# Second block, attention: the last head rows' 1/rms moved behind the second and third heads' maxima, and its spreading products one and two heads later

## The chip, the cores and the metric

One core of one Trainium2 chip runs the whole program. The metric is device time in microseconds (us) of one execution; less is better. TensorE multiplies matrices into PSUM (PE in the profile, its weight loads are PEld), VectorE (DVE) and ScalarE (ACT) do the elementwise work and the activations, GpSimd (POOL) makes the low halves of split weights, and SyncE (SP) issues the loads of the weight stream.

## The reference

Two transformer-like blocks run on a sequence of 256 rows with 1024 columns. The change lies in the second block's attention, whose 16 heads are 64 wide: 8 "forgetting" heads (fox) and 8 "stick breaking" heads (sb).

```python
q, k, v = heads(proj...)                  # (16 heads, 256, 64)
q_fox = rms_norm_2(q[:, :8], fox_q_g)     # x * rsqrt(mean(x*x) + eps) * g, per head and row
k_fox = rms_norm_2(k[:, :8], fox_k_g)
...
logits = q_fox @ k_fox.T * scale + cum_f[q] - cum_f[k]      # causal
p = softmax(logits);  o_fox = p @ v
o = concat([o_fox, o_sb]) @ w_out
h = h + o
```

So before any logit of a fox head can be made, the head's query and key must have been divided by their root mean square, 8 query and 8 key heads in all, held as blocks of two heads (128 partitions).

## The kernel before

Each engine has its own instruction queue, written out by hand in program order, and the engines meet at counting semaphores. Work is staged: first block, its feed-forward part, then the second block's attention (its part here is from about 645 us to 750 us of the span), and then the feed-forward and convolution parts.

In the attention, TensorE projects 16 blocks `j` of queries and keys (`project`). The square sums of blocks 4g to 4g+3 are collected as 8 rows (`head_sums`, L1038, group g). Their 1/rms is made in two parts: ScalarE forms a first guess by logarithm and exponential (`row_rsqrt(g)`, L1588 and L1591), and VectorE improves it in one Newton step of four operations on 8x256 elements (`row_rstd(g)`, L1761 to L1765). The result is split into a high part by ScalarE (`heads_hi(g)`, L1596) and a low part by VectorE (`heads_lo(g)`, L2276). TensorE then spreads the rows over 128 partitions, one product of 256 columns per block (`spread_rstd(i)`, L1048, block i of 16), and VectorE multiplies block i by it (`finish_qk(i)`, L2283). Group 3, the one that the change moves, belongs to blocks 12 to 15, and these are the queries and keys of fox heads 4 to 7.

The spreads of blocks 12 and 14 write one PSUM bank, those of 13 and 15 another. `spread_rstd(14)` therefore waits for `finish_qk(12)`, and `spread_rstd(15)` for `finish_qk(13)`.

Each fox head h then goes through this chain:

- `fox_scores(h)`, TensorE: two query tiles, products L1147, L1149, L1151 and L1153. It waits for its blocks (`qk_fin`) and for the exponentials of head h-2.
- `fox_maximum(h)`, VectorE: two reductions, L2346.
- `fox_exps(h)`, ScalarE: two activations with sums, L1651.
- `fox_even(h)`, VectorE: a reciprocal (L2352) and two multiplications (L2355).
- `fox_transposes(h)`, TensorE: three transposes, L1165.
- `fox_turned(h)`, VectorE: a copy out of PSUM, L2363.
- `fox_values(b)`, TensorE: the product with v for heads 2b and 2b+1, L1174 and L1178.

`sb_values(b)` (L1124, L1128) is the corresponding product of the sb heads. `out_hi(n)` on ScalarE (L1642) and `out_lo(n)` on VectorE (L2339) split an output block. `out_half(n, half)` on TensorE (L546 to L548, 12 products) is half of the output projection of block n. `out_half(0, 0)` waits until all 16 blocks are finished (`qk_fin` 26), since it writes the banks of the spreads. It stands behind `fox_scores(4)` in TensorE's queue, and `fox_values(0)` stands behind it.

Four waits are the ones to keep in mind:

```python
# spread_rstd(i)
pe.wait_ge(S["heads_split"], 1 + g)
if i > 8: pe.wait_ge(S["qk_fin"], 10 + fin_before(i) + 1)
# fox_transposes(h)
pe.wait_ge(S["fox_even"], 2 * h + 2)
# out_half(n, 0)
pe.wait_ge(S["qk_fin"], 26)
```

Of the kernel before, what the change touches and what calls it, by code (L numbers as in the profile page):

```python
# [135 lines left out]
def build(nc, xc_d, ccol_d, params_d, const_d, const1_d, const2_d, wgate_d, wf_d, stream_d, out_d):  # L136
# [3 lines left out]
    with ctx:  # L140
# [351 lines left out]
        def q_bank(j):  # L492
            return 2 + j if j < 2 else 4 + j % 2
# [26 lines left out]
        def fin_out(i):  # L520

            return PS[:, 4 + i % 2, T:2 * T] if i < 8 else PS[:, 0 if i < 12 else i % 2, 0:T]

        def fin_before(i):

            return i - 1 if i < 13 else i - 2
# [17 lines left out]
        def _(pe):  # L544
# [496 lines left out]
            def spread_rstd(i):  # L1041

                g, b = i // 4, i % 4
                pe.wait_ge(S["heads_split"], 1 + g)
                pe.wait_ge(S["heads_ready"], 4)
                if i > 8:
                    pe.wait_ge(S["qk_fin"], 10 + fin_before(i) + 1)
                pe.matmul(fin_out(i), spread2[b // 2][:, P * (b % 2):P * (b % 2) + P], head_rows[g],  # L1048
                          start=True, stop=True).then_inc(S["fin_bc"], 1)
# [106 lines left out]
            def fox_transposes(h):  # L1156

                pe.wait_ge(S["fox_even"], 2 * h + 2)
                if h >= 2:
                    pe.wait_ge(S["fox_pt"], h - 1)  # L1160
                else:
                    pe.wait_ge(S["evac_v"], v_before + 20)
                    pe.wait_ge(S["qk_fin"], 10 + 8)
                for k in range(3):
                    mm = pe.transpose(PS[:, 4 + h % 2, P * k:P * k + P], f_P[h % 3][:, P * k:P * k + P], ident)  # L1165
                mm.then_inc(S["ft_done"], 1)
# [16 lines left out]
            def out_half(n, half):  # L1183

                wait_rest(pe, S_OUT2 + n)
                pe.wait_ge(S["t2_lo"], n + 1)
                if half == 0:
                    pe.wait_ge(S["qk_fin"], 26)
                else:
                    pe.wait_ge(S["fox_exp"], 16)  # L1190
                for m in range(4 * half, 4 * half + 4):
                    mm = mm3(PS[:, m // 2, (m % 2) * T:(m % 2) * T + T], *w(S_OUT2 + n, m), *out_rows(n),
                             n == 0 and m % 2 == 0, False)
                if half == 1:
                    mm.then_inc(blk_done, 1)
# [24 lines left out]
            for h in range(2, 11):  # L1220
                if h < 10:
                    fox_transposes(h - 2)
                if h < 8:
                    fox_scores(h)
                if h == 2:
                    sb_values(3)
                if h in (2, 3):
                    spread_rstd(2 * h + 8)
                    spread_rstd(2 * h + 9)
                if 4 <= h < 8:  # L1230
                    out_half(h - 4, 0)
                if h in (8, 9):
                    out_half(h - 8, 1)
                if h in (4, 6, 8, 10):
                    fox_values((h - 4) // 2)
# [34 lines left out]
        def _(act):  # L1270
# [322 lines left out]
            def heads_hi(g):  # L1593

                act.wait_ge(S["rq_done"], 3 + g)
                act.activation(head_rows[g][0:8, :], PS[0:8, g % 2, T:2 * T], ACT.Copy).then_inc(S["heads_hi"], 1)  # L1596
# [47 lines left out]
            def fox_exps(h):  # L1644

                act.wait_ge(S["fox_max"], 2 * h + 2)
                if h >= 3:
                    act.wait_ge(S["ft_done"], h - 2)
                for qt, cols in enumerate(FOX_Q):
                    u = 2 * h + qt  # L1650
                    act.activation(f_P[h % 3][:, cols], PS[:, 2 + h % 2, cols], ACT.Exp, bias=foxnm[:, u:u + 1],  # L1651
                                   accum_out=foxsum[:, u:u + 1]).then_inc(S["fox_exp"], 1)

            for j in range(18):
                if j == 17:
                    fox_exps(0)
                if j in (5, 9, 13, 17):
                    row_rsqrt((j - 5) // 4)
                if j == 17:
                    sb_weights(7)  # L1660
                    heads_hi(3)
                if 0 <= j - 9 < 8:
                    sb_logs(j - 9)
                if 0 <= j - 10 < 7:
                    sb_weights(j - 10)
                if j in (13, 15, 17):
                    out_hi((j - 13) // 2)
                if j < 16:
                    act.wait_ge(blk_done, S_ATT2 + KC + j + 1)
                    if 6 <= j < 14:  # L1670
                        act.wait_ge(S["fin_bc"], j - 5)
                    if j >= 2:
                        act.wait_ge(S["st_done"], 10 + j - 1)
                    act.activation(sqr2[j % 2], PS[:, q_bank(j), 0:T], ACT.Square).then_inc(S["qk_sq"], 1)
                    if j in (5, 9, 13):
                        heads_hi((j - 5) // 4)
                    if j == 3:
                        fox_operands()
                    if j == 4:
                        act.wait_ge(S["f_add"], 1)  # L1680
                        act.activation(fr[1][0:8, :], fr[0][0:8, :], ACT.Abs).then_inc(S["f_act"], 1)
                        act.wait_ge(S["f_act"], 1)
                        act.activation(fr[1][0:8, :], fr[1][0:8, :], ACT.Exp, scale=-1.0).then_inc(S["f_act"], 1)
                        act.wait_ge(S["f_act"], 2)
                        act.activation(fr[1][0:8, :], fr[1][0:8, :], ACT.Ln, bias=1.0).then_inc(S["f_act"], 1)
                    splits_upto(S_ATT2 + KC + j + RING)


            for h in range(1, 12):
                if h < 8:  # L1690
                    fox_exps(h)
                if h == 3:
                    out_hi(3)
                if h in (5, 7, 9, 11):
                    out_hi(4 + (h - 5) // 2)
# [31 lines left out]
        def _(dve):  # L1727
# [537 lines left out]
            def row_rstd(g):  # L2265
                dve.wait_ge(S["st_done"], 10 + 4 * g + 4)
                r = PS[0:8, g % 2, T:2 * T]
                newton(rr2[1][0:8, :], r, fr[2][0:8, :], r, PS[0:8, g % 2, 0:T],
                       1.0 / HD, S["rq_done"], lambda x: dve.wait_ge(S["row_act"], 4 + 2 * g + 2))
                dve.wait_ge(S["rq_done"], 3 + g)  # L2270

            def heads_lo(g):

                dve.wait_ge(S["heads_hi"], 1 + g)
                r = PS[0:8, g % 2, T:2 * T]
                dve.tensor_tensor(head_rows[g][32:40, :], r, head_rows[g][0:8, :].bitcast(f32), ALU.subtract)\  # L2276
                   .then_inc(S["heads_split"], 1)
# [3 lines left out]
            def finish_qk(i):  # L2281
                dve.wait_ge(S["fin_bc"], i + 1)
                dve.scalar_tensor_tensor(q2[:, i, :], q2[:, i, :], gains[2 * (i // 8) + i % 2], fin_out(i),  # L2283
                                         ALU.mult, ALU.mult).then_inc(S["qk_fin"], 1)
# [50 lines left out]
            def out_lo(n):  # L2335

                dve.wait_ge(S["t2_hi"], n + 1)
                hi, lo = out_rows(n)
                dve.tensor_tensor(lo, PS[:, 6 + n % 2, 0:T], hi.bitcast(f32), ALU.subtract).then_inc(S["t2_lo"], 1)  # L2339

            def fox_maximum(h):

                for qt, cols in enumerate(FOX_Q):
                    u = 2 * h + qt
                    dve.wait_ge(S["fs_done"], 2 * h + 2)
                    dve.tensor_reduce(foxnm[:, u:u + 1], PS[:, 2 + h % 2, cols], AX.X, ALU.max, negate=True)\  # L2346
                       .then_inc(S["fox_max"], 1)
# [52 lines left out]


            finish_qk(11)
            row_rstd(3)
            fox_maximum(1)
            heads_lo(3)
            for h in range(2, 12):
                if h < 10:
                    fox_turned(h - 2)
                if h == 2:
                    fox_maximum(h)  # L2410
                    out_lo(2)
                if h < 9:
                    fox_even(h - 1)
                if 3 <= h < 8:
                    fox_maximum(h)
                if h in (2, 3):
                    finish_qk(2 * h + 8)
                    finish_qk(2 * h + 9)
                if h == 3:
                    out_lo(3)  # L2420
                if h in (5, 7, 9, 11):
                    out_lo(4 + (h - 5) // 2)
# [205 lines left out]
```

## Time and profile before

| | |
|---|---|
| median of 3 runs | 1244.06 us (1242.25 to 1244.53) |
| profiled execution, its own time | 1248.76 us |
| profiled execution, span from first to last instruction | 1247.0 us |
| TensorE busy | 1235.5 us, 99% |
| VectorE busy | 737.0 us, 59% |
| ScalarE busy | 670.9 us, 54% |
| GpSimd busy | 712.3 us, 57% |
| mean granted TensorE clock over the span | 0.994 |

A busy share is the time in which at least one instruction of the engine is in flight. TensorE's matrix products are pipelined, so it counts as busy also where it is not at its peak. The granted clock is 1.00 at 2.4 GHz and 0.50 at 1.2 GHz.

### The profile page before, as it was taken

The numbers are of one execution on the slowest core, as the hardware profiler recorded it, in microseconds if no ns is written. First come the engines' busy times: TensorE is split into PE (matmuls) and PEld (weight loads), VectorE is DVE, ScalarE is ACT, GpSimd is POOL, SyncE is SP. The second block draws the span as 40 slices with busy tenths as digits, with TensorE's granted clock in tenths as the row PEclk, the third lists the DMA queues.
The fourth block names the chain that finished last, engine by engine and source line by source line (L and its number), as shares of the span: only waits on it lengthen the run. The fifth ranks groups of instructions, "written<-read, shape, count | busy, mean of one in ns | idle before, by whom it ended". The sixth has DMA issues, their size and how long they took to land.

```text
span 1247.0 us, 24363 instructions
## 1 busy us (share of the span) xinstructions
PE 1235.5 (99%) x8666; PEld 1109.5 (89%) x8666; DVE 737.0 (59%) x1619; ACT 670.9 (54%) x1205; POOL 712.3 (57%) x308
## 2 busy tenths in 40 slices
PE   8999999999999999999999999999999999999998
PEld 5788889877799999999888779999999999999998
DVE  5796667456542666665626644766666334766665
ACT  6333334455544755555755526666666445666663
POOL 5476553342258656558675306655675986665563
PEclk9999999999999999999999979999999999999999
DMA  9978542231146455456463204554564654555451
GB/s 342 369 257 303 203 152 69 87 110 58 36 135 181 140 188 201 168 185 220 144 186 121 85 1 122 183 186 170 199 217 132 195 185 150 172 202 179 174 218 52
DMA packets 58188, 208.11 MB, mean 167 GB/s; under 512 B 6640, under 2 KB 7808, under 8 KB 58112
## 3 DMA queue, kind: packets, MB, share of 16 engines
q1 hardware_dynamic: 57888, 206.56, 48.7%
q8 instruction: 49, 0.80, 0.3%
q0 software_dynamic: 224, 0.52, 0.1%
q14 instruction: 27, 0.22, 0.1%
HBM read 206.01 MB, written 1.05 MB: 166 GB/s over the span
## 4 chain that ended last, share of the span: by engine, by line
PE 93%; DVE 3%; DMA 1%; ACT 1%; issue 1%; POOL 1%; SPq 0%; DVEq 0%; ACTq 0%
PE ps L546 18%; PE ps L547 18%; PE ps L548 18%; PE ps L575 13%; PE ps L577 6%; PE ps L597 2%; PE ps L599 2%; PE ps L600 2%; PE ps L822 2%; PE ps L627 1%; PE ps L893 1%; PE ps L919 1%; PE ps L908 1%; DMA raw<-in_stream 1%; PE ps L1153 1%
## 5 line engine op out<-in xcount | busy, mean ns | idle before, releaser
L333 POOL TENSOR_TENSOR wlo<-raw,whi 128x1024 fp32r<-128x1024 f32 x287 | 695.7, 2438 | 506.6 <-ACT whi L1283 467.1
L1283 ACT ACTIVATE whi<-raw 128x1024 fp32r<-128x1024 f32 x338 | 353.2, 1054 | 110.7 <-PE ps L548 43.4
L546 PE MATMUL ps<-H,whi 128*128 128x256 f32 (+3 forms) x1312 | 386.5, 295 | 1.4 <-DVE H L1816 1.1
L547 PE MATMUL ps<-H,whi 128*128 128x256 f32 (+3 forms) x1312 | 377.5, 288 | 0.0
L548 PE MATMUL ps<-H,wlo 128*128 128x256 f32 (+3 forms) x1312 | 377.3, 288 | 0.0
L546 PEld LDWEIGHTS ps<-H,whi 128*128 128x128 f32 (+1 forms) x1312 | 250.4, 191 | 14.3 <-issue 10.0
L547 PEld LDWEIGHTS ps<-H,whi 128*128 128x128 f32 (+1 forms) x1312 | 250.9, 191 | 2.5
L548 PEld LDWEIGHTS ps<-H,wlo 128*128 128x128 f32 (+1 forms) x1312 | 250.3, 191 | 2.5
L575 PE MATMUL ps<-H,whi 128*128 128x512 f32 x672 | 238.9, 398 | 0.0
L2205 DVE SCALAR_TENSOR_TENSOR arena<-ps,sm,arena 128x256 f32<-128x256 f32 (+2 forms) x264 | 127.5, 483 | 103.7 <-ACT arena L1541 96.1
L577 PE MATMUL ps<-H,wlo 128*128 128x256 f32 x672 | 188.7, 281 | 0.0
L546 PE MATMUL ps<-dh,whi 128*128 128x256 f32 x584 | 165.4, 283 | 0.5 <-DVE dl L2214 0.5
L547 PE MATMUL ps<-dl,whi 128*128 128x256 f32 x584 | 165.2, 283 | 0.0
L548 PE MATMUL ps<-dh,wlo 128*128 128x256 f32 x584 | 165.2, 283 | 0.0
L575 PEld LDWEIGHTS ps<-H,whi 128*128 128x128 f32 x672 | 126.3, 188 | 29.5
L577 PEld LDWEIGHTS ps<-H,wlo 128*128 128x128 f32 x672 | 127.0, 189 | 0.0
L546 PEld LDWEIGHTS ps<-dh,whi 128*128 128x128 f32 x584 | 111.1, 190 | 2.8 <-POOL wlo L333 0.9
L548 PEld LDWEIGHTS ps<-dh,wlo 128*128 128x128 f32 x584 | 111.3, 191 | 0.0
L547 PEld LDWEIGHTS ps<-dl,whi 128*128 128x128 f32 x584 | 111.3, 191 | 0.0
L1541 ACT ACTIVATE arena<-ps,sm 128x256 f32<-128x256 f32 x132 | 66.1, 500 | 16.6 <-DVE ps L2195 12.8
L1533 ACT ACTIVATE arena<-ps 128x256 f32<-128x256 f32 x84 | 32.3, 385 | 62.4 <-PE ps L577 62.3
L2167 DVE TENSOR_TENSOR wlo<-raw,whi 128x1024 fp32r<-128x1024 f32 x51 | 62.3, 1222 | 1.5 <-issue 0.3
(337 smaller groups left out, 1496.3 us busy)
## 6 DMA issues: line engine op xcount, KB each, us to landing
raw<-in_stream SPq DMA_DIRECT2D x386, 512.0 KB, 4.2
X<-in_xc SPq DMA_DIRECT2D x4, 512.0 KB, 6.0
out_y<-X SPq DMA_DIRECT2D x8, 128.0 KB, 1.9
kx<-in_const SPq DMA_DIRECT2D x1, 512.0 KB, 8.6
params<-in_params SPq DMA_DIRECT2D x1, 344.0 KB, 5.1
kx<-in_const POOLq DMA_DIRECT2D x1, 256.0 KB, 4.3
k<-in_const POOLq DMA_DIRECT2D x1, 129.0 KB, 5.6
k<-in_const SPq DMA_DIRECT2D x1, 128.0 KB, 5.1
```

Source lines behind the costliest of these rows:

```text
L333: pool.tensor_tensor(wlo[:, slot, :], raw[:, rslot, :], whi[:, slot, :].bitcast(f32), ALU.subtract).then_inc(rest_done[0], 1)
L546: pe.matmul(out, lh, rh, start=start, stop=False, skip_group_check=True)
L547: pe.matmul(out, lh, rl, start=False, stop=False, skip_group_check=True)
L548: return pe.matmul(out, ll, rh, start=False, stop=stop, skip_group_check=True)
L575: pe.matmul(PS[:, bank, :], wh_, F[:, k, :, :].rearrange("p h n -> p (h n)"), start=k == 0, stop=False, skip_group_check=True)
L577: mm = pe.matmul(PS[:, bank, T:2 * T], wl_, Fh[:, k, :], start=False, stop=k == KC - 1, skip_group_check=True)
L597: pe.matmul(out, hi[:, k, tok], wh_, start=k == 0 and first, stop=False, skip_group_check=True)
L1283: act.activation(whi[:, s % RING, :], raw[:, r % RING, :], ACT.Copy).then_inc(hi_done, 1)
L1533: act.activation(tc, PS[:, 4 + 2 * slot + j, T:2 * T], ACT.Copy).then_inc(S["half_out"], 1)
L1541: act.activation(tc, PS[:, 4 + 2 * slot + j, at:at + T], ACT.Identity, bias=bias, scale=taps_of(f)[:, slot, 3 * j:3 * j + 1]).then_inc(S[" ...
L2167: dve.tensor_tensor(wlo[:, s % RING, :], raw[:, RAW_OF_W[s] % RING, :], whi[:, s % RING, :].bitcast(f32), ALU.subtract).then_inc(rest_done ...
L2205: dve.scalar_tensor_tensor(tc[:, lo:hi], u[:, src:src + hi - lo], taps_of(f)[:, slot, 3 * j + 1 + n:3 * j + 2 + n], tc[:, lo:hi], ALU.mult ...
```

## The change

The Newton step of group 3 (`row_rstd(3)`) leaves its place ahead of `fox_maximum(1)` on VectorE and goes behind `fox_maximum(2)` and `out_lo(2)`. `heads_hi(3)` on ScalarE goes from ahead of `fox_exps(1)` to behind `fox_exps(2)`. `heads_lo(3)` goes to head step h = 3, behind `fox_turned(1)`. On VectorE `fox_even(1)` now stands ahead of `fox_maximum(2)`. On TensorE the spreads of blocks 12 and 13 go from step 2 to the same place in step 3, behind `fox_scores(3)`, and those of 14 and 15 from behind `fox_scores(3)` to step 4, between `fox_transposes(2)` and `fox_scores(4)`. `finish_qk(12)` and `(13)` go from step 2 to step 3, behind `fox_maximum(3)`; `finish_qk(14)` and `(15)` go from step 3 to step 4, behind `fox_turned(2)`. No instruction is added or removed.

```diff
 # TensorE
             for h in range(2, 11):
                 if h < 10:
                     fox_transposes(h - 2)
+                if h == 4:
+                    spread_rstd(14)
+                    spread_rstd(15)
                 if h < 8:
                     fox_scores(h)
                 if h == 2:
                     sb_values(3)
-                if h in (2, 3):
-                    spread_rstd(2 * h + 8)
-                    spread_rstd(2 * h + 9)
+                if h == 3:
+                    spread_rstd(12)
+                    spread_rstd(13)
                 if 4 <= h < 8:
                     out_half(h - 4, 0)
 # ScalarE
                 if j == 17:
                     sb_weights(7)
-                    heads_hi(3)
...
             for h in range(1, 12):
                 if h < 8:
                     fox_exps(h)
+                if h == 2:
+                    heads_hi(3)
                 if h == 3:
                     out_hi(3)
 # VectorE
             finish_qk(11)
-            row_rstd(3)
             fox_maximum(1)
-            heads_lo(3)
             for h in range(2, 12):
                 if h < 10:
                     fox_turned(h - 2)
-                if h == 2:
-                    fox_maximum(h)
-                    out_lo(2)
+                if h == 3:
+                    heads_lo(3)
+                if h == 4:
+                    finish_qk(14)
+                    finish_qk(15)
                 if h < 9:
                     fox_even(h - 1)
-                if 3 <= h < 8:
+                if h < 8:
                     fox_maximum(h)
-                if h in (2, 3):
-                    finish_qk(2 * h + 8)
-                    finish_qk(2 * h + 9)
+                if h == 2:
+                    out_lo(2)
+                    row_rstd(3)
                 if h == 3:
+                    finish_qk(12)
+                    finish_qk(13)
                     out_lo(3)
```

## Rows read from the trace of the kernel before

**Rows 1.** The page: span, busy TensorE, and the chain that ended last, by engine.

```profile
span 1247.0 us, 24363 instructions
PE 1235.5 (99%) x8666; PEld 1109.5 (89%) x8666; DVE 737.0 (59%) x1619; ACT 670.9 (54%) x1205; POOL 712.3 (57%) x308
...
PE 93%; DVE 3%; DMA 1%; ACT 1%; issue 1%; POOL 1%; SPq 0%; DVEq 0%; ACTq 0%
```

**Rows 2.** Windows (from:to, length, busy us by engine with counts, granted clock, DMA).

```profile
706.00:719.00 13.00, 12.84 (x74) 8.80 (x73) 10.20 (x27) 6.87 (x20) 2.36 (x1) 1.00 0.14 41
...
720.00:734.00 14.00, 14.00 (x56) 10.73 (x56) 6.09 (x20) 2.10 (x9) 0.00 (x0) 0.51 0.00 1
734.00:751.00 17.00, 17.00 (x125) 13.94 (x125) 7.47 (x24) 3.89 (x16) 0.00 (x0) 1.00 0.00 1
```

**Rows 3.** The chain that ended last, at 712 us (start, us, what).

```profile
712.04 0.91 ACT arena L1651 x4
```

**Rows 4.** Timeline of VectorE (start, us, instruction, idle before it and its releaser).

```profile
714.59 0.48 DVE L2283 SCALAR_TENSOR_TENSOR arena<-arena,params,ps 128x256 f32<-128x256 f32 x1
714.98 0.40 DVE L1761 TENSOR_SCALAR arena<-ps 8x256 f32<-8x256 f32 x1
...
716.75 0.62 DVE L2346 TENSOR_REDUCE sm<-ps 128x1 f32<-128x128 f32 x2
717.40 0.41 DVE L2276 TENSOR_TENSOR H<-ps,H 8x256 fp32r<-8x256 f32 x1
717.85 0.56 DVE L2363 COPY arena<-ps 128x384 f32<-128x384 f32 x1
718.32 0.61 DVE L2346 TENSOR_REDUCE sm<-ps 128x1 f32<-128x128 f32 x2
718.85 0.41 DVE L2339 TENSOR_TENSOR H<-ps,H 128x256 fp32r<-128x256 f32 x1
719.18 0.15 DVE L2352 RECIPROCAL sm<-sm 128x2 f32<-128x2 f32 x1
...
724.06 0.62 DVE L2346 TENSOR_REDUCE sm<-ps 128x1 f32<-128x128 f32 x2 [2.02 <-PE ps L1153]
```

**Rows 5.** Timeline of ScalarE.

```profile
716.75 0.38 ACT L1596 ACTIVATE H<-ps 8x256 fp32r<-8x256 f32 x1 [2.67 <-DVE ps L1765]
...
718.97 0.37 ACT L1651 ACTIVATE arena<-ps,sm 128x128 f32<-128x128 f32 x1 [0.65 <-DVE sm L2346]
```

**Rows 6.** Timeline of TensorE.

```profile
715.01 0.70 PE L1153 MATMUL ps<-arena 64*128 64x256 f32 x2
...
717.92 0.65 PE L1124 MATMUL ps<-arena 128*64 128x256 f32 x4
...
718.72 0.50 PE L1048 MATMUL ps<-H 40*128 40x256 f32 x2
719.98 0.80 PE L1165 MATMUL ps<-k,arena 128*128 128x128 f32 x3 [0.76 <-DVE arena L2355]
...
724.50 0.45 PE L1147 MATMUL ps<-dh,dl 128*128 128x128 f32 x1
...
728.02 0.58 PE L546 MATMUL ps<-H,whi 128*128 128x256 f32 x1
...
730.88 1.12 PE L1174 MATMUL ps<-arena 128*64 128x256 f32 x4
...
736.80 0.49 PE L1165 MATMUL ps<-k,arena 128*128 128x128 f32 x3
737.05 0.31 PE L1147 MATMUL ps<-dh,dl 128*128 128x128 f32 x1
...
739.03 0.39 PE L546 MATMUL ps<-H,whi 128*128 128x256 f32 x1
...
740.66 0.65 PE L1174 MATMUL ps<-arena 128*64 128x256 f32 x4
...
741.46 0.55 PE L1165 MATMUL ps<-k,arena 128*128 128x128 f32 x3
```

## The prediction

> **What bounds the kernel now.** I read the page first, for the engine that sets the time: TensorE, 99% busy and 93% of the chain that ended last, with VectorE at 3% [rows 1]. So a change on VectorE or ScalarE pays only where TensorE really stands still or where its clock changes, and the reader should look for those two things. Second come the windows. From 706 to 719 us TensorE runs at the full clock, from 720 to 734 us at a mean of 0.51, from 734 us on at 1.00 again [rows 2]; a mean of 0.51 over these 14 us is 0.49 / 0.50 x 14 = 13.7 us at 0.50, about 720.1 to 733.8. Third the timelines of the three engines around the fall. TensorE stands still for 0.76 us ahead of `fox_transposes(1)` at 719.98, released by VectorE's normalisation of head 1 [rows 6]. That normalisation is late because four operations of the Newton step, from 714.98 to 716.75, stand ahead of `fox_maximum(1)` [rows 4], although scores(1) had ended at 715.01 + 0.70 = 715.71 [rows 6]. Everything behind scores(4) in this stage is TensorE's own work, so what scores(4) loses or gains the end of the kernel loses or gains, apart from the clock.
>
> **What is removed ahead of head 1.** Nothing is removed or added; queue places change. The Newton step is 716.75 - 714.98 = 1.77 us [rows 4]. `fox_maximum(1)` can't start at once in its place, since its scores end at 715.71; I put it at 715.75, a gain of 1.0 us. Its exponentials start 0.65 us later (718.32 to 718.97) [rows 4, 5], at 716.40, and take 0.91 [rows 3], to 717.3. Before, `heads_hi(3)` took ScalarE from 716.75 [rows 5]; that was hidden under the maximum, so moving it is worth nothing by itself. VectorE does turned(0) at 716.40 for 0.47 (717.85 to 718.32) and is idle until even(1) at 717.35, since even(1) now stands ahead of maximum(2). From the reciprocal to the released transposes it is 719.98 - 719.18 = 0.80 [rows 4, 6], so they may go at 718.15. But TensorE has scores(2) until 717.92 and `sb_values(3)` until 718.72 [rows 6]: transposes(1) start at 718.72. That is 1.26 us earlier, and the idle time there is gone. The two spreads that stood at 718.72 (0.50 us for both) had lain inside that idle stretch and had been free.
>
> **What is moved behind it, at the full clock.** Steps on TensorE: transposes 0.25 and scores 1.98 (736.80, 737.05, 739.03) [rows 6]. Scores(3) end at 718.72 + 2.23 = 720.95. Now the spreads of 12 and 13 want `heads_lo(3)`. On VectorE maximum(2) starts at 717.35 + 0.75 = 718.10 (0.20 for the reciprocal, as 719.18 to 719.38, and about 0.55 for two multiplications, an estimate from the 0.80 above), out_lo(2) 0.53 later (718.32 to 718.85), the Newton step 0.33 after that (718.85 to 719.18) [rows 4], at 718.96, to 720.73. `heads_hi(3)` follows at once, as at 716.75 [rows 5], hidden under turned(1) (0.47), and `heads_lo(3)` (717.40 to 717.85, 0.45 [rows 4]) ends at about 721.65. What is queued behind the waiting spread on TensorE is transposes(2), and behind these all the rest.
>
> - Spreads 12 and 13 start at 721.7: TensorE idle for 0.75, then 0.50 of work, to 722.2.
> - Even(2) starts at 721.65, so transposes(2) at 722.45: idle 0.25, then 0.25 of work, to 722.7.
> - Maximum(3) takes VectorE from 722.40 to 723.05 (0.65, as 716.75 to 717.40), then come finish(12) and finish(13), 0.39 apart (714.59 to 714.98) and 0.48 long [rows 4]. Spread 14 waits for the first: 723.55, idle 0.85. Spread 15 waits for the second: 723.95, idle some 0.15, and done at 724.2.
> - Scores(4) start at 724.2. `out_half(0, 0)` waits for finish(15): out_lo(3) can go at about 724.25 (exponentials(3) from 723.05 + 0.65, less the overlap of their tail, and a 0.4 copy), then turned(2), finish(14), finish(15), done at about 725.95. Scores(4) end at 726.2, so this wait is covered, with 0.25 to spare. Without this cover it is a cost of its own, below.
>
> Before, at a full clock, transposes(1) at 719.98, 2.23, 0.50 for two spreads (14 and 15) and 0.25 for transposes(2) give scores(4) at 722.95; even(2) was no later than that. So the sum at the full clock is -1.26 (earlier start) + 0.50 (spreads 12 and 13, now behind it) + 2.0 (0.75 + 0.25 + 0.85 + 0.15 of waits) = +1.25 us.
>
> **The clock.** The profiled execution had scores(4) at 724.50 [rows 6], not at 722.95, since the clock had fallen at 720.1. Scores take 728.02 - 724.50 = 3.52 at half clock against 1.98, `out_half` 730.88 - 728.02 = 2.86 against 740.66 - 739.03 = 1.63 [rows 6], about 1.78 times as long. A low clock costs nothing in front of a wait, and that is what decides here.
>
> - If it falls again at 720.1: scores(3) has 1.15 us done and ends at 721.6, spreads end at 722.6, transposes(2) at 723.05, and the two waits for finish(12) and (13) are the same, spread 15 goes at 723.95 and scores(4) at 724.4. Against 724.50 that is -0.1 us. The lower end.
> - If it falls behind the new waits, at about 723.5, for as long as before (13.7 us), the low stretch lies over scores(4) 3.52, `out_half(0, 0)` 2.86, values(0) 1.42 (0.80 x 1.78; 740.66 to 741.46), head 5's transposes and scores 3.97 and part of the next half, and scores(6) start at 738.5 instead of 737.05 [rows 6]: +1.4 us. The upper end.
>
> The change fills the idle time that preceded the fall and opens a wider thin stretch, 720.95 to 724.2, with 2.0 us of waits in 3.25 us. I therefore lean to the later fall, and take +1.0, between the ends and nearer to the upper one.
>
> **Two rules beside it.** By the Trainium skill ("TensorE: Matmul & The Clock Gate", Part 2, Step-by-step), only weight loads are pulled ahead, and "the MATMULs themselves stay in program order". It speaks against this change: a spread that waits holds transposes(2) and scores(4) behind it. With passing allowed, the 2.0 us of waits would go and the sum would be -0.8. The trace's TensorE timeline has every product in program order around 719.98 [rows 6]. The same page (A second HAM failure mode) says that micro-idles between groups of products make the clock swing. The trace agrees so far that it fell behind a stretch whose longest idle time shown was 0.76 us; by that rule the fall stays after the change.
>
> **The rivals.**
>
> 1. *The spreads stay hidden.* VectorE is quicker than I sum, scores(4) wait for nothing new, and the 1.26 us of head 1 are kept: 1242.8. For it: ScalarE and VectorE have idle time here (2.02 us ahead of maximum(3) at 724.06 [rows 4]). Against: the Newton step, turned(1), heads_lo, even(2) and maximum(3) in a row are work, 4.1 us from 718.96, and nothing overlaps them.
> 2. *The clock does not fall after the change.* Scores(4) at 724.2 and 1.98 + 1.63 + 0.80 + 0.25 + 1.98 + 1.63 + 0.25 = 8.52 behind it give scores(6) at 732.7 instead of 737.05, -4.3: 1239.7, faster. For it: the idle time of 0.76 is gone. Against: there is more idle time just behind it. It decides if TensorE's thin stretch from 721 to 724 no longer brings the clock down.
> 3. *A fall that the timed executions of before did not have* (slower). The profiled execution's own time is 4.7 us above the median of the runs shown, which is of the size of one fall. If the timed ones keep the clock, before has scores(6) at 722.95 + 8.52 = 731.5, and the new waits bring the fall in: 738.5, +7.0: 1251.1. It decides if the timed executions of before kept their clock over the 0.76 us of idle time and those of after lose it over the new waits. Against: the thin products from 706 on are the same in every execution.
> 4. *The finishes slip.* If finish(15) comes 1.5 us later than I sum, `out_half(0, 0)` waits for it beyond the 0.25 of cover, +1.25 on top of +1.25: +2.5, 1246.6.
>
> **How the numbers follow.** The sum is made against the profiled execution (1248.76 us, span 1247.0) and its difference carried over to the median of 1244.06, which has no trace; all that follows scores(4) is the same work. Forecast 1244.06 + 1.0 = 1245.1, chance 0.67; rival 1 0.10; rival 2 0.08; rival 3 0.08; rival 4 0.07. A difference within 0.2%, 2.5 us, can hardly be told from no change here, as the three runs lie 2.3 us apart. Faster is rival 2 and a little of rival 1, 0.09; the same is the forecast and most of rival 1, 0.76; slower is rival 3, most of rival 4 and the forecast's tail, 0.15. The forecast's own -0.1 to +1.4, with some 1.2 us for the scatter of a median, rival 1's -1.3 and rival 4's +2.5 give 1241.5 to 1248.0; rivals 2 and 3 are left out.
>
> **What the profile after would show.** Right: maximum(1) at about 715.75 and transposes(1) at about 718.7 without idle time ahead of them; TensorE waiting for VectorE (L2276) ahead of the first spread, and again (L2283) ahead of the third; scores(4) within 0.4 us of 724.3; a granted clock of 0.50 for some 13.7 us that starts between 720 and 724 us. Wrong: a clock of 1.00 throughout (rival 2), no wait of TensorE in 721 to 724 us (rival 1), or `out_half(0, 0)` waiting for L2283 (rival 4). What I could most easily have wrong is where the clock falls, since it is worth more than all the waits.

## The result: slower, by 4.5 us

| | before | after |
|---|---|---|
| median | 1244.24 us (6 runs, 1242.25 to 1247.08) | 1248.74 us (6 runs, 1247.09 to 1249.50) |
| ratio | | 1.0038, 95% interval 1.0025 to 1.005 |
| profiled execution, span | 1247.0 us | 1247.1 us |
| mean granted clock over that span | 0.994 | 0.997 |

The first thing to see is that the two profiled spans are alike and the medians are not. The profiled execution of before, at 1248.76 us, was slower than all six timed ones, and the forecast of 1245.1 us was built on it.

The profile after: TensorE's waits from 706 to 751 us (engine, line, releaser: us in total, times, longest). L1048 are the spreads, L1165 the transposes, L2280 the low part of group 3 (L2276 before), L2287 the finishes (L2283 before), L2359 the normalisation (L2355 before).

```profile
PE ps L1048 <- DVE H L2280: 0.6, 1, 0.6
PE ps L1048 <- DVE arena L2287: 0.5, 1, 0.5
PE ps L1165 <- DVE arena L2359: 0.3, 1, 0.3
PE ps L1147 <- issue: 0.2, 1, 0.2
```

Before there was one such wait, 0.76 us ahead of the transposes of head 1 [rows 6]. It is gone, and three others have taken its place. TensorE's timeline after shows them:

```profile
717.44 0.31 PE L1147 MATMUL ps<-dh,dl 128*128 128x128 f32 x1
...
719.42 0.65 PE L1124 MATMUL ps<-arena 128*64 128x256 f32 x4
719.90 0.39 PE L1128 MATMUL ps<-arena 128*64 128x128 f32 x4
720.22 0.55 PE L1165 MATMUL ps<-k,arena 128*128 128x128 f32 x3
...
721.89 0.70 PE L1153 MATMUL ps<-arena 64*128 64x256 f32 x2
723.23 0.50 PE L1048 MATMUL ps<-H 40*128 40x256 f32 x2 [0.65 <-DVE H L2280]
724.01 0.55 PE L1165 MATMUL ps<-k,arena 128*128 128x128 f32 x3 [0.28 <-DVE arena L2359]
725.02 0.91 PE L1048 MATMUL ps<-H 40*128 40x256 f32 x2 [0.47 <-DVE arena L2287]
725.87 0.47 PE L1147 MATMUL ps<-dh,dl 128*128 128x128 f32 x1
...
737.13 0.31 PE L1147 MATMUL ps<-dh,dl 128*128 128x128 f32 x1
```

What to see: the transposes of head 1 follow `sb_values(3)` without a gap, 2.78 us behind the start of scores(2) (717.44 to 720.22). Behind scores(3) the spread of block 12 waits for the low part, the transposes wait for the normalisation, the spread of block 14 waits for the finish of block 12. All of these stand in one VectorE queue:

```profile
720.07 0.42 DVE L2343 TENSOR_TENSOR H<-ps,H 128x256 fp32r<-128x256 f32 x1
720.40 0.40 DVE L1765 TENSOR_SCALAR arena<-ps 8x256 f32<-8x256 f32 x1
...
722.17 0.56 DVE L2367 COPY arena<-ps 128x384 f32<-128x384 f32 x1
722.76 0.41 DVE L2280 TENSOR_TENSOR H<-ps,H 8x256 fp32r<-8x256 f32 x1
723.21 0.17 DVE L2356 RECIPROCAL sm<-sm 128x2 f32<-128x2 f32 x1
723.41 0.55 DVE L2359 TENSOR_SCALAR arena<-arena,sm 128x128 f32<-128x128 f32 x2
723.87 0.62 DVE L2350 TENSOR_REDUCE sm<-ps 128x1 f32<-128x128 f32 x2
724.41 0.47 DVE L2287 SCALAR_TENSOR_TENSOR arena<-arena,sm,ps 128x256 f32<-128x256 f32 x1
```

From the first operation of the Newton step at 720.40 to the first finish at 724.41 VectorE goes from one operation to the next with next to no pause: it is busy for 1.90 and 1.87 us of the first two windows of 2 us below. Windows of the same stretch (columns as in [rows 2]):

```profile
720.00:722.00 2.00, 2.00 (x18) 1.56 (x15) 1.90 (x6) 0.92 (x4) 0.00 (x0) 1.00 0.00 0
722.00:724.00 2.00, 1.08 (x4) 0.47 (x4) 1.87 (x7) 0.37 (x1) 0.00 (x0) 1.00 0.00 0
724.00:726.00 2.00, 1.48 (x6) 0.88 (x6) 1.53 (x5) 1.19 (x5) 0.00 (x0) 0.86 0.04 8
726.00:728.00 2.00, 2.00 (x7) 1.66 (x8) 1.97 (x7) 0.00 (x0) 0.00 (x0) 0.50 0.00 0
...
732.00:734.00 2.00, 2.00 (x17) 1.39 (x17) 0.36 (x1) 0.00 (x0) 0.00 (x0) 0.93 0.00 0
```

TensorE is busy for 1.08 us of the 2 us from 722, and at 725.4 the clock falls to 0.50. It comes back at 732.3: (0.14 + 3 x 0.50 + 0.07) x 2 / 0.50 = 6.8 us at half clock, over scores(4) and the first half block, up to the start of `fox_values(0)`.

Since each execution reaches this stage a microsecond earlier or later, I measure from the start of scores(2) (the L1147 at 717.44 here, at 715.93 in the profiled execution of before) to that of scores(4) and of scores(6). After: 725.87 - 717.44 = 8.43 and 737.13 - 717.44 = 19.69 us.

### The profile page after: what moved, and what is told of

It is laid out like the page before. It is cut to its first block, busy times and chain, and to the rows that moved or that the text cites. A ratio compares the mean times of both kernels' runs of the same rounds, so it can differ in the third digit from the quotient of the medians.

```text
span 1247.1 us, 24363 instructions
## 1 busy us (share of the span) xinstructions
PE 1233.3 (99%) x8666; PEld 1107.4 (89%) x8666; DVE 735.2 (59%) x1619; ACT 670.5 (54%) x1205; POOL 712.1 (57%) x308
## 4 chain that ended last, share of the span: by engine, by line
PE 93%; DVE 3%; DMA 2%; ACT 1%; issue 1%; POOL 0%; SPq 0%; DVEq 0%; ACTq 0%
PE ps L546 18%; PE ps L547 18%; PE ps L548 18%; PE ps L575 13%; PE ps L577 6%; PE ps L597 2%; PE ps L599 2%; PE ps L600 2%; PE ps L822 2%; PE ps L627 1%; PE ps L893 1%; PE ps L919 1%; DMA raw<-in_stream 1%; PE ps L908 1%; PE ps L1153 1%
```

## The experiments

Eleven runs, in three groups, each beside before on the group's own chip, so that ratios to before can be compared across groups and bare times can't. The mean granted clock of each execution is listed with its time, and it became the most useful number. It is a mean over the whole span: it tells how much low clock an execution had, not where. 6.8 us at half clock make it 0.997, 3.4 us make it 0.999. So 0.997 or less is some 6 us of low clock or more (called a long fall below), 1.000 is next to none, and 0.998 or 0.999 can hide a short fall, or a low clock behind TensorE's last product, where it costs nothing (0.77 from 1240 us on in before_again, with TensorE done at 1239). Only the profiled executions show the place.

### 1. before_again: what do before's executions look like?

The kernel before, no edit.

> The kernel before itself, unchanged, as the measure of scatter and of the clock in its executions. Theory 1 (the clock): most of its executions keep the clock through the second attention, so their mean granted clock over the span is 0.998 or more (the end of the span alone costs about 0.001), and the long fall of the profiled execution (0.994) is the exception. Theory 2 (work and waits alone): falls are as frequent here as in the changed kernel, 0.995 to 0.997, and the 4.5 us come from elsewhere. Both expect a ratio of 1.000 within 0.0015.

Measured: 1242.96 us, ratio 0.9997 (0.9987 to 1.0006). The 11 executions have a mean clock of 0.998 to 1.000. Over all 100 executions of before in the three groups 88 are at 0.998 or more and 59 at 1.000, and only 12 lie at 0.993 to 0.997; those at 1.000 have a median of 1242.9 us, those at 0.993 to 0.996 took 1247.0 to 1249.7 us. The 12 are spread unevenly: 1 of 43, 7 of 35 and 4 of 22 in the three groups. Of the changed kernel's 18 executions (these 6 and the 12 of after_again) every one is at 0.995 to 0.997. So before's profiled execution, at 0.994 and 1248.76 us, belonged to a small minority. TensorE's timeline of before_again's profiled execution (1243.88 us, clock 0.998):

```profile
717.09 0.31 PE L1147 MATMUL ps<-dh,dl 128*128 128x128 f32 x1
...
721.13 0.55 PE L1165 MATMUL ps<-k,arena 128*128 128x128 f32 x3 [0.75 <-DVE arena L2355]
...
722.80 0.50 PE L1048 MATMUL ps<-H 40*128 40x256 f32 x2
723.12 0.38 PE L1153 MATMUL ps<-arena 64*128 64x256 f32 x1
723.42 0.55 PE L1165 MATMUL ps<-k,arena 128*128 128x128 f32 x3
723.72 0.31 PE L1147 MATMUL ps<-dh,dl 128*128 128x128 f32 x1
...
732.21 0.31 PE L1147 MATMUL ps<-dh,dl 128*128 128x128 f32 x1
```

and its window:

```profile
720.00:734.00 14.00, 13.25 (x88) 10.41 (x88) 9.67 (x33) 4.20 (x18) 0.00 (x0) 1.00 0.00 1
```

The same 0.75 us of idle time is there, and the clock stays at 1.00. The low clock that its mean of 0.998 tells of lies elsewhere in the span:

```profile
228.00:230.00 2.00, 2.00 (x10) 1.00 (x9) 1.97 (x6) 0.28 (x1) 0.00 (x0) 1.00 0.02 8
230.00:232.00 2.00, 2.00 (x14) 2.00 (x13) 1.72 (x6) 1.89 (x7) 0.00 (x0) 0.65 0.00 0
232.00:234.00 2.00, 2.00 (x9) 1.78 (x9) 1.97 (x5) 1.99 (x2) 0.00 (x0) 0.50 0.00 0
```

That is 3.4 us at half clock at 230.6 us, and the trace shows TensorE busy throughout and waiting for no engine from 215 to 245 us. So a fall can also come without a wait; the experiments below show what waits do in the second attention, not the whole cause of falls.

In the second attention scores(4) start 6.63 us behind scores(2), scores(6) 15.12 us. Against this the change costs 19.69 - 15.12 = 4.57 us in this stage alone, about the measured 4.5. Against the profiled execution of before (737.05 - 715.93 = 21.12 us [rows 6]) it would have been a gain of 1.43 us.

### 2. after_fill: the same waits, with TensorE busy in them

```diff
+            def filler(n, bank):
+                if bank == 6:
+                    pe.wait_ge(S["t2_lo"], 3)
+                for _ in range(n):
+                    pe.matmul(PS[:, bank, T:T + P], ones, ident, start=True, stop=True, ...)
...
                 if h == 4:
+                    filler(2, 6)
                     spread_rstd(14)
...
                 if h == 3:
+                    filler(3, 6)
                     spread_rstd(12)
                     spread_rstd(13)
+                    filler(1, 6)
```

> The changed kernel with six unused 128-column products of full rows put into TensorE's queue where it stood still: three ahead of the spread of block 12, one behind that of block 13, two ahead of that of block 14. The waits stay, TensorE is busy in them. Theory 1: no fall of the clock, mean 0.998 or more, and only the waits' 1.25 us against before: ratio 1.001 (1.000 to 1.002). Theory 2: nothing changes or it gets a little slower: 1.0036 to 1.0045.

Measured: 1244.54 us, ratio 1.0012 (1.0003 to 1.0021), 11 executions at 0.999 to 1.000. Eight of them are at 1.000, where all 18 of the changed kernel are at 0.995 to 0.997. Work was added, and the kernel became faster than the change: 1.0012 beside 1.0038, and 1.0030 in after_again. The window, and TensorE's timeline (L1202 are the unused products):

```profile
720.00:734.00 14.00, 13.96 (x93) 11.05 (x91) 9.27 (x29) 4.27 (x19) 0.00 (x0) 1.00 0.00 1
```

```profile
716.96 0.31 PE L1147 MATMUL ps<-dh,dl 128*128 128x128 f32 x1
...
722.03 0.94 PE L1202 MATMUL ps<-k 128*128 128x128 f32 x6
722.89 0.50 PE L1048 MATMUL ps<-H 40*128 40x256 f32 x2
...
725.22 0.33 PE L1147 MATMUL ps<-dh,dl 128*128 128x128 f32 x1
...
733.71 0.31 PE L1147 MATMUL ps<-dh,dl 128*128 128x128 f32 x1
```

The distances are 8.26 and 16.75 us. So of the 4.57 us, 16.75 - 15.12 = 1.63 are the new order with its waits, all of it ahead of scores(4) (8.26 - 6.63), and 19.69 - 16.75 = 2.94 are the clock.

### 3. before_fill: such products in before's own wait

```diff
+                if h == 2:
+                    filler(3, 0)
                 if h in (2, 3):
                     spread_rstd(2 * h + 8)
```

> The kernel before with three such products ahead of the spread of block 12, inside the 0.76 us of idle time ahead of the transposes of head 1. Theory 1: the timed executions had no fall, so nothing changes: 1.000 within 0.001, and no profiled fall at 720 us. Theory 2, if before has the fall as often as after: its falls go and it gets faster by up to 0.4% (0.996).

Measured: 1243.27 us, 1.0000 (0.9991 to 1.0009), 11 executions at 0.998 to 1.000. The fillers had next to nothing to win, since of the 32 executions of before beside them only one is below 0.998. Whether they would take away before's rare falls this run can't show.

### 4. late_spreads: the late half of the change alone

The changed kernel, but `row_rstd(3)` ahead of `fox_maximum(1)`, `heads_hi(3)` behind `sb_weights(7)` and `heads_lo(3)` behind `fox_maximum(1)`, where before has them.

> The late half of the change alone: spreads and finishes of blocks 12 to 15 as in the changed kernel, but the Newton step, the high and the low part of group 3 where the kernel before has them. The first spread has then nothing to wait for; those of blocks 14 and 15 still wait for the finishes of 12 and 13 behind the third head's maximum. By the sum scores(4) come 1.0 us later than before at the full clock. Theory 1: 1.001 if the clock holds, 1.003 or more if the remaining waits (0.5 us longer ahead of head 1, 0.5 us ahead of scores(4)) bring a fall. Theory 2: 1.001, and the rest of the 4.5 us lies in the Newton step's place.

Measured: 1246.36 us, 1.0023 (1.0014 to 1.0033), eight of ten executions at 0.996 or 0.997. Its trace has a wait of 0.7 us for the finish of block 12 (here L2286) and 0.4 us ahead of head 1, scores(4) 7.45 us behind scores(2), and a clock of 0.76 from 720 to 734 us:

```profile
722.63 0.74 PE L1048 MATMUL ps<-H 40*128 40x256 f32 x2 [0.72 <-DVE arena L2286]
```

The late place of the spreads and finishes is enough for a fall in most executions. The sum had scores(4) 1.0 us later than before; it is 7.45 - 6.63 = 0.8.

### 5. after_again: the change itself, with the next three

> The changed kernel unchanged, on the chip on which the next three run. Theory 1 (waits of 1.5 us and a clock fall of about 3 us that the timed executions of before do not have): ratio 1.0036 to 1.0048, mean granted clock 0.995 to 0.997 in nearly all executions, against 0.998 or more in before's. Theory 2 (waits alone, and the 4.5 us were scatter): 1.0012 to 1.002.

Measured: 1248.36 us, 1.0030 (1.0019 to 1.0041), a little below the expected 1.0036. Seven of the 35 executions of before beside it had a long fall too (0.994 to 0.997), which draws the ratio down; the two medians are 4.5 us apart (1248.36 and 1243.86). All 12 of its own are at 0.995 to 0.997. The waits alone, 1.0012 to 1.002, are excluded by the executions' clock; the ratio's interval begins at 1.0019 and does not exclude them.

### 6. before_wait: one wait, nothing moved

```diff
+                if h == 4:
+                    pe.wait_ge(S["qk_fin"], 26)
                 if h < 8:
                     fox_scores(h)
```

> The kernel before with nothing moved, only one wait added: scores(4) wait until all 16 blocks are finished, some 1.2 us longer. Theory 1: the wait itself is worth 1.2 us (1.0010) and the fall comes in at about 724 us, 3 us more: 1.003 to 1.004, mean clock 0.997. Theory 3, that the fall comes from the moved work and not from TensorE standing still: 1.001, clock 0.999.

Measured: 1247.35 us, 1.0024 (1.0013 to 1.0034); three executions at 0.996, six at 0.997, three at 0.999. TensorE's timeline:

```profile
720.75 0.55 PE L1165 MATMUL ps<-k,arena 128*128 128x128 f32 x3 [0.76 <-DVE arena L2357]
...
724.60 0.33 PE L1147 MATMUL ps<-dh,dl 128*128 128x128 f32 x1 [1.01 <-DVE arena L2285]
```

The added wait leaves TensorE idle for 1.01 us and scores(4) start 7.90 us behind scores(2), 1.27 later than in before. The profiled execution had a short fall, 3.4 us at half clock, though its mean over the span is 0.999; by their means nine of the other 11 had longer ones:

```profile
720.00:734.00 14.00, 12.24 (x71) 9.30 (x72) 7.86 (x27) 3.17 (x16) 0.00 (x0) 0.88 0.00 1
```

One more wait, with nothing moved, does to before most of what the whole change does (nine of 12 executions at 0.997 or below, against 18 of 18). So the moved work is not needed for the fall.

### 7. wait_fill: that wait, filled

```diff
                 if h == 4:
+                    filler(5, 6)
                     pe.wait_ge(S["qk_fin"], 26)
```

> The kernel before with the added wait of before_wait, and five unused 128-column products of full rows ahead of that wait, about as long as it. Theory 1 (the clock falls because TensorE stands still): no fall, mean clock 0.999 or more, 1.0010. Theory 3 (it falls for another reason, such as when scores(4) run): as before_wait, 1.0024.

Measured: 1244.93 us, 1.0005 (0.9991 to 1.0018), ten of 11 executions at 0.999 or 1.000 (five of each). Scores(4) start 7.89 us behind scores(2), as in before_wait, and the window reads:

```profile
720.00:734.00 14.00, 13.83 (x95) 11.26 (x96) 8.55 (x29) 3.36 (x15) 0.00 (x0) 1.00 0.01 1
```

The interval of the ratio overlaps that of before_wait, so the ratio alone would not settle it; the clocks do: one execution of 11 at 0.997 or below, against nine of 12. The unused products both end the standing still and add work. Which of the two keeps the clock up no run here separates: none puts such products anywhere but into a wait.

### 8. fill_first and fill_second: which of the waits?

fill_first keeps only `filler(3, 6)` and `filler(1, 6)` of after_fill, fill_second only `filler(2, 6)`.

> The changed kernel with the unused products only around the first wait (three ahead of the spread of block 12, one behind that of block 13); the wait ahead of spreads 14 and 15 stays idle. If the first wait is the one that brings the fall: no fall, 1.0012. If the fall wants both waits to be idle, the same. If the second wait suffices: 1.0035 to 1.0045, clock 0.997. I expect the first or second of these, since the longer idle time is here.

> The changed kernel with the unused products only ahead of the spread of block 14, two of them; the first wait of 0.65 us and the 0.28 us behind it stay idle. If the fall wants both waits: 1.0012. If the first suffices: 1.0035 to 1.0045. I expect a mixture here, 1.002 to 1.004, with the fall in some executions and not in others.

Measured: fill_first 1246.33 us, 1.0016 (1.0004 to 1.0028), four executions each at 0.997, 0.999 and 1.000. fill_second 1248.02 us, 1.0027 (1.0015 to 1.0040), ten of 12 at 0.995 to 0.997. Neither expectation held cleanly. By the means, eight executions of 12 have no long fall with the first wait filled, and two of 12 with the second. The profiled execution of fill_first has one wait left in this stage, of 0.40 us, and a short fall all the same:

```profile
PE ps L1048 <- DVE arena L2296: 0.4, 1, 0.4
720.00:734.00 14.00, 13.56 (x74) 10.29 (x75) 8.60 (x27) 2.87 (x14) 0.00 (x0) 0.88 0.01 1
```

Beside before_again, which kept its clock over 0.75 us, this shows that the length of the waits does not settle the matter for a single execution. They change how often the clock falls and for how long; what decides in a single execution I can't tell from these runs.

### 9. newton_mid: the Newton step whole behind the first maximum

`row_rstd(3)` directly behind `fox_maximum(1)`, `heads_hi(3)` behind `fox_exps(1)`, `heads_lo(3)` behind `fox_even(1)`; the rest as in the change.

> The changed kernel with the Newton step whole behind the maximum of head 1, the high part behind its exponentials and the low part behind its normalisation; spreads and finishes late as in the change. The wait ahead of the spread of block 12 goes (the low part is ready 2 us early), but the normalisation of head 1 is 0.7 us late again, and the spread of block 14 still waits for finish(12) behind the third maximum. Sum by the timelines: scores(4) some 1.3 us later than in before. With a fall in most executions 1.0020 to 1.0025 (as late_spreads), without 1.001.

Measured: 1247.01 us, 1.0032 (1.0020 to 1.0044), five of six executions at 0.996 or 0.997, and slower than expected (1.0020 to 1.0025). TensorE's waits in its trace are these:

```profile
PE ps L1165 <- DVE arena L2359: 1.0, 2, 0.5
PE ps L1048 <- DVE arena L2287: 0.5, 1, 0.5
```

The wait for the low part is gone as expected, but two waits of 0.5 us for normalisations and one of 0.5 us for the finish are there, and the clock is at 0.76 from 720 to 734 us. Scores(4) start 7.89 us behind scores(2), 1.26 later than in before, as the sum said (1.3). The rest of the 4 us by which it is slower (0.0032 of 1243) I put down to the clock; no filled version of this kernel was run.

### 10. interleaved: the Newton step in VectorE's holes

Operations one and two of `row_rstd(3)` stand ahead of the maximum, three and four behind it. ScalarE's `heads_hi(3)` stands behind `fox_exps(1)`. The edit is shown against before, the helper `row_rstd_parts` left out.

```diff
 # VectorE
             finish_qk(11)
-            row_rstd(3)
+            parts = row_rstd_parts(3)
+            next(parts)
             fox_maximum(1)
-            heads_lo(3)
+            next(parts)
...
                     fox_turned(h - 2)
-                if h == 2:
-                    fox_maximum(h)
-                    out_lo(2)
+                if h == 3:
+                    finish_qk(12)
+                    finish_qk(13)
                 if h < 9:
                     fox_even(h - 1)
-                if 3 <= h < 8:
+                if h == 2:
+                    heads_lo(3)
+                if h < 8:
                     fox_maximum(h)
-                if h in (2, 3):
-                    finish_qk(2 * h + 8)
-                    finish_qk(2 * h + 9)
+                if h == 2:
+                    out_lo(2)
+                if h == 3:
+                    finish_qk(14)
+                    finish_qk(15)
 # TensorE
+                if h == 3:
+                    spread_rstd(12)
+                    spread_rstd(13)
                 if h < 8:
                     fox_scores(h)
...
-                if h in (2, 3):
-                    spread_rstd(2 * h + 8)
-                    spread_rstd(2 * h + 9)
+                if h == 3:
+                    spread_rstd(14)
+                    spread_rstd(15)
```

> A version meant to beat both: two operations of the Newton step ahead of the first head's maximum, in VectorE's hole while scores(1) still run, two behind it; high part behind the first head's exponentials, low part behind its normalisation; the spreads of 12 and 13 directly behind the transposes of head 1, the rest as before. By the timelines the transposes of head 1 go at 718.7 instead of 720.0 and no wait takes the place of that: scores(4) 0.3 to 0.7 us earlier than in before, and less for the clock to fall on. Theory 1: 0.9990 to 0.9997, clock 1.000 in more of the executions than in before's. If the moved spreads wait for the low part: 1.000.

Measured: 1242.37 us, 0.9996 (0.9987 to 1.0005), eight of 11 executions at 1.000. Its trace shows no wait of TensorE for another engine from 706 to 751 us:

```profile
716.11 0.31 PE L1147 MATMUL ps<-dh,dl 128*128 128x128 f32 x1
...
718.90 0.55 PE L1165 MATMUL ps<-k,arena 128*128 128x128 f32 x3
719.37 0.50 PE L1048 MATMUL ps<-H 40*128 40x256 f32 x2
...
722.23 0.31 PE L1147 MATMUL ps<-dh,dl 128*128 128x128 f32 x1
...
730.70 0.31 PE L1147 MATMUL ps<-dh,dl 128*128 128x128 f32 x1
```

Scores(4) start 6.12 us behind scores(2), 0.51 earlier than in before, as expected. It beats the changed kernel (at most 1.0005 beside before, where the change is at least 1.0019); against before the gain of half a microsecond is in the trace but inside the scatter of the times. Whether its clock holds more often than before's is not shown either: three of 11 executions are at 0.998 or 0.999, and none of 11 below that, against four of the 22 of before beside it.

## Why the prediction was wrong, step by step

- **Removed ahead of head 1: right.** I put the transposes of head 1 at 718.72, 2.79 us behind scores(2); they came 2.78 us behind. The idle time ahead of them is gone.
- **Moved behind it, at the full clock: right.** I put scores(4) at 724.2, 8.27 us behind scores(2); after_fill, whose clock stayed up, has 8.26. Behind scores(2) the first spread was put at 5.77 us and came at 5.79, the transposes of head 2 at 6.52 and 6.57, the spread of block 14 at 7.62 and 7.58. The profile's idle times (0.65, 0.28, 0.47) are shorter than mine (0.75, 0.25, 0.85 and 0.15) where it counts from the end of the last product in flight, 0.55 us for the transposes, and I counted from the 0.25 after which the next could have started.
- **The sum at the full clock was mis-sized: +1.25, measured +1.63.** The error is on the side of before. I gave its spreads of 14 and 15 a place of 0.50 us behind scores(3). At a full clock they run in among the last products of scores(3) (722.80 beside 723.12 in before_again): scores(4) 6.63 us behind scores(2), not 722.95 - 715.93 = 7.02.
- **The clock: this step failed.** I wrote that the sum "is made against the profiled execution" and "its difference carried over to the median of 1244.06, which has no trace". Both ends of my forecast, -0.1 and +1.4, therefore took a fall in before for granted, and only asked where the one after would lie. The timed executions of before mostly have no long one (88 of 100 at 0.998 or more), so the whole of the fall after is an extra cost: 2.94 us that the forecast had at nothing. The fall's length was wrong as well: I gave the one after the 13.7 us of before's, and it lasted 6.8. With that length the same sum against the profiled execution is -1.43 us and the forecast 1244.06 - 1.43 = 1242.6, further off still: this error hid a part of the first one. The warning stood in the first table: 1248.76 us for the profiled execution beside three runs of at most 1244.53.
- **Rival 3 was what happened**, at a chance of 0.08: "a fall that the timed executions of before did not have". It priced +7.0 us; the measured +4.57 is less, since the fall after lasted 6.8 us and not 13.7, which gives 2.94 us for the clock in place of the 7.0 - 1.25 = 5.8 that it held. My argument against it, that the thin products from 706 us on are the same in every execution, held for the products. It said nothing of the idle time: with the waits filled the long falls are gone in all 11 executions of after_fill.
- **Rivals 1, 2 and 4 did not happen.** TensorE waits for new things, so the spreads do not stay hidden; the clock falls; and `out_half(0, 0)` follows scores(4) at 729.40 without a wait for the finishes.
- **The rule on products in order** (the Trainium skill, "TensorE: Matmul & The Clock Gate", Part 2, Step-by-step) spoke against the change, and the trace agrees where it matters: the waiting spread at 723.23 held the transposes and scores behind it. The trace does not agree for a product that is ready: in before_again the spreads of blocks 14 and 15, which stand behind scores(3) in the queue, start at 722.80, and the second of the two records of the last product of scores(3) starts at 723.12. They cost nothing there: from the transposes ahead of scores(3) to the next product behind them it is 2.29 us with two spreads among them (721.13 to 723.42) and 2.29 us without any (719.74 to 722.03 in after_fill). With the other rule of that page, on micro-idles between groups (A second HAM failure mode), the trace agrees: the longest idle time after was 0.65 us, and filling the gaps took the long fall away. I had quoted it for the fall staying, where it should have been read as the fall coming.

## What to carry to other kernels

A profile is one execution: compare its own time and granted clock with the timed runs before pricing anything by it, and if it lies outside them ask which of its features the others lack. Where an engine's work is thin already, moving small work from in front of one wait into the next stretch of the queue can cost more than its waits; here an order that was 1.6 us longer at the full clock cost 4.6. Where small links of a chain have to go, the holes that other waits leave on their own engine are worth a try: in interleaved this took away every wait of the stage, though the time against before did not move beyond its scatter.

## What was not expected of the hardware

The same code falls or keeps its clock from one execution to the next, and the falls have different lengths: at this place 3.4 us in before_wait's profiled execution, 6.8 in the changed kernel's, 13.7 in the one of before. With one wait of 0.75 us in this stretch 12 executions of 100 had a mean clock of 0.997 or below; with one more wait of 1.01 us some 3 us later it was nine of 12. And five products whose results nobody reads, put into that wait, made the kernel faster: 1.0005 beside before in place of 1.0024, about 2.4 us. In before_again's profiled execution the clock fell at 230.6 us with TensorE busy and waiting for no engine.
